# Output projection in three fp32r products at each weight chunk, with the routing of both token tiles in one piece behind it

## The chip, the cores and the metric

The kernel runs on one core of a Trainium2 chip, in one launch. The metric is device time in microseconds. A core has TensorE (PE; its weight loads are listed as PEld), VectorE (DVE), ScalarE (ACT), GpSimd (POOL) and SyncE (SP), which here only issues transfers. Each runs its own instructions in order, and they meet at semaphores. TensorE writes PSUM, eight banks of 512 fp32 columns, named `ps`.

## The reference, cut to what matters

256 tokens of width 1024 go through two layers. Layer 0 mixes tokens with a sparse attention of three branches, layer 1 with a block-sparse one; both end in a product with a 1024 x 1024 matrix, the output projection. After it come a layer norm, a router and a mixture of 16 experts, each token going to two of them.

```python
for layer in range(DEPTH):
    mix = mixer(x, w_in[layer], ...)            # ends in: o @ w_out
    x = layer_norm(DN_ALPHA * x + mix, ln_g[layer, 0], ln_b[layer, 0])
    ffn = grouped_moe(x, router_w, router_bias, w_gate[layer], w_up[layer], w_down[layer])
    x = layer_norm(DN_ALPHA * x + ffn, ln_g[layer, 1], ln_b[layer, 1])
```

`grouped_moe` takes the sigmoid of 16 router scores, picks the best of four groups by the sum of its two best biased scores, and in it the two best experts.

## The kernel before

Tokens lie in two tiles of 128 (index `a` or `t`, `T = 2`). A weight matrix is cut into units of 512 output columns (`UNIT`); a unit has eight chunks of 128 input rows (`KJ = 8`, index `j`). Weights pass through `ring`, eight slots of 2 MB, in the order of `STREAM`: the units of layer 0 (the output projection is units 5 and 6), 48 expert tiles, the units of layer 1 (output projection 13 and 14), 48 expert tiles. SyncE issues the load of an entry when the entry eight places earlier is used up (`wait_consumed`). For the first expert pairs this means: tiles 0 to 5 take slots of input units, tiles 6 and 7 those of the output projection, and tile 8 waits for `main.gate_done`, the end of the first pair's gate product.

**Input projection** (`project`). Operands are split in a high and a low fp32r part. For each chunk, ScalarE copies the weights to `wh` (`split_hi`), VectorE subtracts to get `wl` (`split_lo`), and TensorE makes three products for each token tile: high x high, high x low, low x high. `wh` and `wl` have three buffers (`WBUF`). `xh` and `xl` hold the split input.

**Attention** runs over items `m` (16 in layer 0, two to a pair of heads; 8 in layer 1, one to a pair). On TensorE, iteration `m` has `scores(m)`, `transpose_probs(m-2)` and `times_v(m-3)`. VectorE does the row maximum (`attention_max`, line 1128), `coefficients(m-1)`, one copy of the transposed probabilities (line 1344), and, when a pair of heads is finished, the copy of its output to `OT` (line 1352). ScalarE does four exponentials with sums (line 943) and the other copy of the transposed probabilities (line 952). GpSimd scales the probabilities (lines 1021 and 1022).

**Output projection** (`mix_out`, line 562) multiplies `OT` and the ring's weights as fp32, each matmul being two instructions of 512 columns, on top of a `seed` with the residual (line 569). Six chunks of the first unit come before the last head's `times_v`; then the rest of tile 0, then tile 1. Between the products of tile 1, TensorE transposes tile 0's normed rows (`transpose_tile`) and makes its router scores (`logits`, line 575):

```python
mix_out(l, 1, 0, range(KJ))
transpose_tile(0, R.xt, 4, lambda w: pe.wait_ge(N.x_ready, ready(2 * l, 0, w)))
mix_out(l, 1, 1, range(0, 4))
logits(l, 0)
mix_out(l, 1, 1, range(4, KJ))
```

**Routing** of a tile: VectorE takes statistics of each half row (`half_stats`, line 1173) and norms (`layer_norm`, lines 1177 to 1192, with a power on GpSimd, line 1026); ScalarE rounds the rows to `Xp[0]` (line 956) and GpSimd makes the low part `Xp[1]` (line 1031); both copy transposed rows; ScalarE makes the sigmoid (line 963); VectorE picks groups and experts (`choose`, lines 1204 to 1212), makes gate values (`gate_values`), turns counts of TensorE (`count_before`) into places (`places`) and writes a one-hot matrix `Pm`, a view of `wh[:, 0]` (`one_hot_tile`, line 1227). TensorE then gathers the rows (`gather_tile`, line 593), tile 0 first, tile 1 later, into the same banks, and the first expert pair's gate product follows (`to_hidden`, line 612).

Of the kernel before, what the change touches and what calls it, by code (L numbers as in the profile page):

```python
# [90 lines left out]
def build(nc, x, consts, w_in0, w_out0, cmp_kw1, cmp_kw2, cmp_vw1, cmp_vw2, cmp_kpos, cmp_vpos,  # L91
          w_in1, w_out1, router_w, router_b, w_gate, w_up, w_down, ln_g, ln_b, out):
    ctx = ExitStack()
    with ctx:
# [34 lines left out]
        def tiny(n):  # L129
# [5 lines left out]
        OT = [R6[:, 1536 + j * S:1536 + (j + 1) * S] for j in range(6)] + [R5[:, 2304 + j * S:2304 + (j + 1) * S] for j in range(2)]  # L135
# [68 lines left out]
                              "pt pt_sb pv ot_sb mix ln_in")  # L204
# [3 lines left out]
                   coef=16, scaled=16, pt=16, pt_sb=32, pv=16, ot_sb=8, mix=4, ln_in=32)]  # L208
# [9 lines left out]
        RT = namedtuple("RT", "xt xt_sb logits score sel pos hot table over xp xl ln_in")  # L218
        R = RT(*(sem(f"route_{n}") for n in RT._fields))
        rbase = [RT(*[0] * len(RT._fields)), RT(xt=4, xt_sb=4, logits=T, score=T, sel=T, pos=T, hot=1, table=1, over=1,  # L220
# [27 lines left out]
        def wait_consumed(eng, what):  # L248
# [13 lines left out]
        GATES = 5 * KJ  # L262
        chunk = lambda u, j: u * KJ + j if u < 5 else GATES + 1 + (u - 7) * KJ + j

        def wait_buffer(eng, c):
# [3 lines left out]
            if c == GATES:  # L269
                eng.wait_ge(L.proj, 11)  # L270
                return
            l, v, j = (0, c // KJ, c % KJ) if c < GATES else (1, (c - GATES - 1) // KJ, (c - GATES - 1) % KJ)
            if j == KJ - 1:
                eng.wait_ge(L.proj, base[l].proj + 2 * (v + 1))
            else:
                eng.wait_ge(w_used, (5 * l + v) * (KJ - 1) + j + 1)
# [132 lines left out]
        def _(pe):  # L409
# [125 lines left out]
            def attention(l):  # L535
                n = len(ITEMS[l])
                for m in range(n + 3):
# [6 lines left out]
                    else:  # L544
                        mix_out(l, 0, 0, range(0, 6))
# [9 lines left out]
            def mix_out(l, a, w, js):  # L555
                B, u = base[l], OUT[2 * l + w]
                for j in js:
                    if a == 0 and w == 0:
                        pe.wait_ge(L.ot_sb, B.ot_sb + j + 1)
                    if a == 0 and j % 4 == 0:  # L560
                        pe.wait_ge(*landing(("unit", u), j // 4))
                    last = mm(ps[:, 2 * a + w, :], OT[j][:, a * P:(a + 1) * P],  # L562
                              in_slot(("unit", u))[:, j * UNIT:(j + 1) * UNIT],
                              start=False, stop=(j == KJ - 1), skip_group_check=True)
                if j == KJ - 1:
# [853 lines left out]
```

## Time and profile before

| what | value |
|---|---|
| time, median of 3 runs | 820.42 us (819.17 to 820.86) |
| the profiled execution | 817.06 us, span 815.3 us |
| mean granted TensorE clock | 0.965 |
| TensorE, VectorE, ScalarE, GpSimd busy | 93%, 35%, 23%, 11% |
| HBM read | 243.35 MB |

The trace is one execution. In a row of a window the engines stand in the order PE, PEld, DVE, ACT, POOL. All times of events are microseconds from the start of its span. A matmul's listed duration overlaps that of its neighbours, so a rate is read from start to start. The granted clock is a share of 2.4 GHz and takes two levels, 1.00 and 0.50.

### The profile page before, as it was taken

Reading aid. Unit: us, or ns where it says so; the run is one execution under the profiler, and the core shown is the slowest. Engines: PE = TensorE matmul, PEld = TensorE weight load, DVE = VectorE, ACT = ScalarE, POOL = GpSimd, SP = SyncE. Lnnn points to the kernel's source line nnn. Section 1 sums busy time; section 2 is a strip of 40 time slices with the busy share of each in tenths; the row PEclk is TensorE's granted clock in tenths of the full one; section 3 lists DMA queues with packets and bytes.
Section 4 is the critical chain, followed back from the end, with each engine's and each line's share of the span. In section 5 each row is a group of like instructions: output and inputs, shape, how many; then the busy total and the mean of one; then the engine's idle time right before and its main releaser. Section 6 shows DMA issues by size and latency. Waiting matters only on the chain.

```text
span 815.3 us, 9027 instructions
## 1 busy us (share of the span) xinstructions
PE 754.2 (93%) x3713; PEld 402.3 (49%) x3713; DVE 282.5 (35%) x564; ACT 187.8 (23%) x435; POOL 88.0 (11%) x96
## 2 busy tenths in 40 slices
PE   5999999998999999998878999899899999998884
PEld 4877855545434444343236887555634344443331
DVE  3594365326212211111146874523521122111114
ACT  3443456312111001100004445612200110011000
POOL 0011234312000000000000320411200000000000
PEclk9999789999999999999997999999899999999997
DMA  9999400106599999999999854013489999999981
GB/s 297 366 391 411 188 1 2 52 15 243 201 430 427 428 429 426 428 427 427 429 388 386 328 207 174 34 52 110 148 353 427 428 428 425 430 427 428 428 347 53
DMA packets 38924, 245.03 MB, mean 301 GB/s; under 512 B 5344, under 2 KB 9568, under 8 KB 26592
## 3 DMA queue, kind: packets, MB, share of 16 engines
q1 hardware_dynamic: 38880, 244.41, 74.2%
q8 instruction: 32, 0.52, 0.3%
q14 instruction: 12, 0.10, 0.0%
HBM read 243.35 MB, written 1.05 MB: 300 GB/s over the span
## 4 chain that ended last, share of the span: by engine, by line
PE 79%; DMA 8%; DVE 7%; ACT 3%; issue 2%; POOL 0%; DVEq 0%; SPq 0%
PE ps L612 24%; PE ps L630 12%; DMA ring<-in_w_up 8%; PE ps L562 7%; PE ps L435 5%; PE ps L436 4%; PE ps L437 4%; PE ps L602 3%; PE ps L640 3%; PE ps L484 2%; ACT R L943 2%; PE ps L472 2%; PE ps L593 1%; PE ps L569 1%; PE ps L418 1%
## 5 line engine op out<-in xcount | busy, mean ns | idle before, releaser
L612 PE MATMUL ps<-ring,R 128*64 128x512 f32 x1024 | 229.9, 602 | 17.4 <-DMA ring<-in_w_up 7.9
L612 PEld LDWEIGHTS ps<-ring,R 128*64 128x64 f32 x1024 | 75.4, 138 | 150.6 <-issue 149.0
L630 PE MATMUL ps<-ring,R 128*64 128x512 f32 x512 | 113.4, 595 | 3.1 <-DVE R L1241 3.1
L841 ACT ACTIVATE wh<-ps,small 128x512 fp32r<-128x512 f32 x32 | 22.0, 687 | 276.1 <-PE ps L630 274.5
L1078 DVE TENSOR_TENSOR wl<-ring,wh 128x512 fp32r<-128x512 f32 x88 | 66.5, 770 | 48.3 <-ACT wh L819 48.1
L435 PE MATMUL ps<-wh,xh 128*128 128x512 f32 x176 | 71.9, 409 | 5.0 <-DVE wl L1078 4.9
L436 PE MATMUL ps<-wl,xh 128*128 128x512 f32 x176 | 70.4, 400 | 0.0
L437 PE MATMUL ps<-wh,xl 128*128 128x512 f32 x176 | 70.4, 400 | 0.0
L630 PEld LDWEIGHTS ps<-ring,R 128*64 128x64 f32 x512 | 35.3, 137 | 69.6 <-issue 64.0
L819 ACT CAST wh<-ring 128x512 fp32r<-128x512 f32 x88 | 54.3, 621 | 58.3 <-PE ps L437 58.3
L1249 DVE SCALAR_TENSOR_TENSOR wl<-ps,small,wh 128x512 fp32r<-128x512 f32 x32 | 24.0, 751 | 104.3 <-ACT wh L841 103.6
L562 PE MATMUL ps<-ring,R 128*128 128x512 f32 x128 | 56.8, 597 | 0.0
L1238 DVE TENSOR_TENSOR R<-R,ps 128x512 f32<-128x512 f32 x16 | 17.2, 1075 | 114.3 <-PE ps L612 114.3
L1245 DVE TENSOR_SCALAR wl<-ps 128x256 fp32r<-128x256 f32 x16 | 6.8, 424 | 115.4 <-PE ps L618 115.4
L943 ACT ACTIVATE R<-ps,small 128x128 f32<-128x128 f32 (+1 forms) x96 | 39.0, 419 | 29.7 <-DVE small L1128 29.7
L435 PEld LDWEIGHTS ps<-wh,xh 128*128 128x128 f32 x176 | 33.8, 192 | 15.0 <-DVE xl L1073 4.9
L986 POOL TENSOR_TENSOR R<-wh,small 128x512 f32<-128x512 f32 x8 | 8.3, 1043 | 284.6 <-PE ps L618 272.0
L437 PEld LDWEIGHTS ps<-wh,xl 128*128 128x128 f32 x176 | 33.6, 191 | 8.2
L436 PEld LDWEIGHTS ps<-wl,xh 128*128 128x128 f32 x176 | 33.8, 192 | 7.7
L562 PEld LDWEIGHTS ps<-ring,R 128*128 128x128 f32 x128 | 23.7, 190 | 27.6 <-issue 26.8
L1128 DVE TENSOR_REDUCE small<-ps 128x2 f32<-128x256 f32 (+1 forms) x48 | 24.5, 553 | 35.7 <-PE ps L472 35.7
L1011 POOL TENSOR_TENSOR R<-R 128x512 f32<-128x512 f32 (+1 forms) x16 | 23.3, 1459 | 123.9 <-DVE R L1121 123.9
(152 smaller groups left out, 812.9 us busy)
## 6 DMA issues: line engine op xcount, KB each, us to landing
ring<-in_w_gate SPq DMA_DIRECT2D x32, 2048.0 KB, 18.7
ring<-in_w_up SPq DMA_DIRECT2D x32, 2048.0 KB, 20.1
ring<-in_w_down SPq DMA_DIRECT2D x32, 2048.0 KB, 22.5
ring<-in_w_in SPq DMA_DIRECT2D x22, 1024.0 KB, 14.0
ring<-in_w_out SPq DMA_DIRECT2D x8, 1024.0 KB, 14.9
ring<-in_cmp_kw SPq DMA_DIRECT2D x2, 1024.0 KB, 16.3
ring<-in_cmp_vw SPq DMA_DIRECT2D x2, 1024.0 KB, 13.3
R<-in_ln_g SPq DMA_DIRECT2D x4, 512.0 KB, 5.1
```

Source lines behind the costliest of these rows:

```text
L435: mm(to, xh[:, j, tok], wh[:, c % WBUF], start=(j == 0), stop=False)
L436: mm(to, xh[:, j, tok], wl[:, c % WBUF], start=False, stop=False)
L437: last = mm(to, xl[:, j, tok], wh[:, c % WBUF], start=False, stop=(j == KJ - 1))
L562: last = mm(ps[:, 2 * a + w, :], OT[j][:, a * P:(a + 1) * P], in_slot(("unit", u))[:, j * UNIT:(j + 1) * UNIT], start=False, stop=(j == KJ ...
L602: last = mm(ps[:, bank, at * n:(at + 1) * n], Xp[k][:, a, j, :], Pm[:, a].rearrange("p e c -> p (e c)")[:, 0:n], start=(a == 0 and k == 0) ...
L612: last = mm(ps[64 * e:64 * e + 64, to, :], xe[:, j, at + 64 * e:at + 64 * e + 64], slots[e][:, j * UNIT:(j + 1) * UNIT], start=(j == 0), s ...
L630: last = mm(ps[64 * e:64 * e + 64, 2 + w, :], hT[:, k, 64 * e:64 * e + 64], slots[e][:, at:at + UNIT], start=(k == 0), stop=(k == FJ - 1))
L640: last = mm(ps[:, 4 + 2 * a + w, :], PmT[:, b, a, :], Yp[k][w], start=False, stop=(k == 1), skip_group_check=True)
L819: copy(wh[:, c % WBUF], in_slot(("unit", u))[:, j * UNIT:(j + 1) * UNIT]).then_inc(w_hi, 1)
L943: last = nc.scalar.activation(to, ps[:, 2 * (m % 2) + a, c:c + w], ACT.Exp, bias=nmax[:, m % 2, t, a:a + 1], accum_out=sums[:, m % 3, t, a ...
L1078: tt(wl[:, c % WBUF], in_slot(("unit", u))[:, j * UNIT:(j + 1) * UNIT], wh[:, c % WBUF], ALU.subtract).then_inc(w_lo, 1)
L1128: last = nc.vector.tensor_reduce(nmax[:, m % 2, t, :], ps[:, b:b + 2, t * P:t * P + (t + 1) * P], AX.X, ALU.max, negate=True)
```

## The change

The output projection is made like the input projection: weights split chunk by chunk in `wh` and `wl`, attention outputs split in two, three fp32r products for both token tiles at each chunk. `OT` is no longer fp32 space of its own but `xh` and `xl`. ScalarE writes the high part of a pair of heads (`out_hi`), VectorE the low part. The first three weight chunks are split during the last attention items. Three chunks (in place of six) come before the last `times_v`. A ring slot of an output unit is free when its last chunk is split. Tile 0 is transposed and routed behind all products; `choose`, `gate_values` and `places` work on both tiles at once, and the gathers of both tiles are in one piece (`gather`, which existed). `gather_tile`, `one_hot_tile` and the semaphore `hot` are gone.

```diff
-        OT = [R6[:, 1536 + j * S:1536 + (j + 1) * S] for j in range(6)] + [R5[:, 2304 + j * S:2304 + (j + 1) * S] for j in range(2)]
+        OT = [xh, xl]
...
-            elif n in OUT:
-                l, w = divmod(OUT.index(n), 2)
-                eng.wait_ge(L.mix, base[l].mix + T + w + 1)
             else:
                 eng.wait_ge(w_lo, chunk(n, KJ - 1) + 1)
...
-                        mix_out(l, 0, 0, range(0, 6))
+                        mix_out(l, 0, range(0, 3))
...
-            def mix_out(l, a, w, js):
+            def mix_out(l, w, js):
                 B, u = base[l], OUT[2 * l + w]
                 for j in js:
-                    if a == 0 and w == 0:
+                    c = chunk(u, j)
+                    if w == 0:
                         pe.wait_ge(L.ot_sb, B.ot_sb + j + 1)
-                    if a == 0 and j % 4 == 0:
-                        pe.wait_ge(*landing(("unit", u), j // 4))
-                    last = mm(ps[:, 2 * a + w, :], OT[j][:, a * P:(a + 1) * P],
-                              in_slot(("unit", u))[:, j * UNIT:(j + 1) * UNIT],
-                              start=False, stop=(j == KJ - 1), skip_group_check=True)
-                if j == KJ - 1:
-                    last.then_inc(L.mix, 1)
+                    pe.wait_ge(w_lo, c + 1)
+                    for a in range(T):
+                        to, tok = ps[:, 2 * a + w, :], slice(a * P, (a + 1) * P)
+                        mm(to, OT[0][:, j, tok], wh[:, c % WBUF], start=False, stop=False, skip_group_check=True)
+                        mm(to, OT[0][:, j, tok], wl[:, c % WBUF], start=False, stop=False, skip_group_check=True)
+                        last = mm(to, OT[1][:, j, tok], wh[:, c % WBUF], start=False, stop=(j == KJ - 1), skip_group_check=True)
+                        if j == KJ - 1:
+                            last.then_inc(L.mix, 1)
+                    if j < KJ - 1:
+                        last.then_inc(w_used, 1)
...
                 attention(l)
-                mix_out(l, 0, 0, range(6, KJ))
-                mix_out(l, 0, 1, range(KJ))
-                mix_out(l, 1, 0, range(KJ))
+                mix_out(l, 0, range(3, KJ))
+                mix_out(l, 1, range(KJ))
                 transpose_tile(0, R.xt, 4, lambda w: pe.wait_ge(N.x_ready, ready(2 * l, 0, w)))
-                mix_out(l, 1, 1, range(0, 4))
                 logits(l, 0)
-                mix_out(l, 1, 1, range(4, KJ))
-                pe.wait_ge(R.sel, C.sel + 1)
-                count_before(0)
                 for w in range(2):
                     seed(4 + w, 0, w, True)
                 transpose_tile(1, R.xt, 6, lambda w: pe.wait_ge(N.x_ready, ready(2 * l, 1, w)))
-                logits(l, 1)
-                pe.wait_ge(R.hot, C.hot + 1)
-                pe.wait_ge(R.xl, C.xl + 2)
-                for bank in range(4):
-                    gather_tile(bank, (2 * bank, 2 * bank + 1), 4 * SLOTS, 0)
+                logits(l, 1).then_inc(R.logits, 1)
                 seed(6, 1, 0, True)
-                pe.wait_ge(R.sel, C.sel + 2)
-                count_before(1)
+                pe.wait_ge(R.sel, C.sel + 1)
+                count_before()
                 pe.wait_ge(R.xl, C.xl + 2 * T)
...
+            def out_hi(l, m):
+                B, nb = base[l], BRANCHES[l]
+                if m >= 4 and (m - 4) % nb == nb - 1:
+                    act.wait_ge(L.pv, B.pv + m - 3)
+                    jq = (m - 4) // nb
+                    copy(OT[0][:, jq], ps[:, 6 + jq % 2, 0:S]).then_inc(L.ot_hi, 1)
...
                         copy(PTb[m % 2][:, 1, :], ps[:, 5, 0:3 * P]).then_inc(L.pt_sb, 1)
+                    out_hi(l, m)
+                    if n - 4 <= m < n - 1:
+                        split_hi(OUT[2 * l], m - n + 4)
+                for m in (n + 2, n + 3):
+                    out_hi(l, m)
+                for w in range(2):
+                    for j in range(3 - 3 * w, KJ):
+                        split_hi(OUT[2 * l + w], j)
...
                     if m >= 4 and (m - 4) % nb == nb - 1:
-                        dve.wait_ge(L.pv, B.pv + m - 3)
                         jq = (m - 4) // nb
-                        copy(OT[jq], ps[:, 6 + jq % 2, 0:S]).then_inc(L.ot_sb, 1)
-                half_stats(0, 0, 0, L.mix, B.mix + 1)
-                step(half_stats(0, 1, 0, L.mix, B.mix + 2))
+                        dve.wait_ge(L.ot_hi, B.ot_hi + jq + 1)
+                        tt(OT[1][:, jq], ps[:, 6 + jq % 2, 0:S], OT[0][:, jq], ALU.subtract).then_inc(L.ot_sb, 1)
+                    if n - 3 <= m < n:
+                        split_lo(OUT[2 * l], m - n + 3)
+                for w in range(2):
+                    for j in range(3 - 3 * w, KJ):
+                        split_lo(OUT[2 * l + w], j)
+                        if w and j == 3:
+                            half_stats(0, 0, 0, L.mix, B.mix + 1)
+                        if w and j == 5:
+                            half_stats(1, 0, 2, L.mix, B.mix + 2)
+                step(half_stats(0, 1, 0, L.mix, B.mix + 3))
                 layer_norm(2 * l, 0, 0, L.ln_in, B.ln_in + 32)
+                step(half_stats(1, 1, 2, L.mix, B.mix + 4))
                 transposed(xTr, 0, R.xt, C.xt, R.xt_sb)
-                half_stats(1, 0, 2, L.mix, B.mix + 3)
-                choose(C, 0)
-                step(half_stats(1, 1, 2, L.mix, B.mix + 4))
                 layer_norm(2 * l, 1, 2, L.ln_in, B.ln_in + 32)
-                places(C, 0)
-                one_hot_tile(0).then_inc(R.hot, 1)
                 transposed(xTr, 1, R.xt, C.xt, R.xt_sb)
-                step(gate_values(C, 0))
-                choose(C, 1)
-                gate_values(C, 1).then_inc(R.table, 1)
-                places(C, 1)
-                one_hot_tile(1).then_inc(main.onehot, 1)
+                choose(C)
+                gate_values(C)
+                places(C)
+                one_hot(main, slice(0, 4), 4)
```

`choose`, `gate_values` and `places` keep their instructions, each now over both tiles; `count_before` keeps its products and makes them together.

## Rows read from the trace of the kernel before

**Rows 1.** One window: length, five engines busy, PEclk, DMA share, GB/s.

```profile
213.00:413.00 200.00, 190.81 (x908) 78.51 (x906) 35.35 (x53) 17.91 (x28) 3.13 (x3) 0.99 1.00 423
```

**Rows 2.** SyncE in order of time; start us, us, line, what is transferred.

```profile
213.06 0.80 SPq L336 DMA_DIRECT2D ring<-in_w_up  x2
```

**Rows 3.** The chain that ended last, in order of time; start us, us, what.

```profile
158.87 5.35 PE ps L562 x12
165.64 15.65 PE ps L562 x36
...
182.16 3.44 PE ps L562 x8
...
187.28 3.54 PE ps L562 x8
190.85 0.71 DVE small L1173
...
196.12 1.96 PE ps L575 x16
...
200.80 1.71 PE ps L569 x2
203.88 2.12 PE ps L593 x16
206.00 7.02 PE ps L612 x32
...
483.11 0.87 PE ps L453 x8
495.18 0.88 PE ps L453 x8
...
569.57 0.71 DVE small L1173
...
574.83 3.60 PE ps L575 x16
...
586.08 7.02 PE ps L612 x32
```

**Rows 4.** Groups of the page: splits of weights, busy us and mean ns.

```profile
L1078 DVE TENSOR_TENSOR wl<-ring,wh 128x512 fp32r<-128x512 f32 x88 | 66.5, 770 | 48.3 <-ACT wh L819 48.1
...
L819 ACT CAST wh<-ring 128x512 fp32r<-128x512 f32 x88 | 54.3, 621 | 58.3 <-PE ps L437 58.3
```

**Rows 5.** ScalarE in layer 1's attention, in order of time.

```profile
524.61 0.37 ACT L943 ACTIVATE R<-ps,small 128x128 f32<-128x128 f32 x1 [1.20 <-DVE small L1128]
...
526.21 0.49 ACT L952 COPY R<-ps 128x384 f32<-128x384 f32 x1
527.59 0.37 ACT L943 ACTIVATE R<-ps,small 128x128 f32<-128x128 f32 x1 [0.89 <-DVE small L1128]
```

**Rows 6.** VectorE in the same stretch; in brackets idle time and releaser.

```profile
525.02 0.42 DVE L1352 COPY R<-ps 128x256 f32<-128x256 f32 x1
526.53 1.02 DVE L1128 TENSOR_REDUCE small<-ps 128x2 f32<-128x256 f32 x2 [1.10 <-PE ps L472]
```

**Rows 7.** VectorE in layer 0's tail, in order of time.

```profile
193.22 1.41 DVE L1192 SCALAR_TENSOR_TENSOR X<-X,small,R 128x512 f32<-128x512 f32 x2
...
200.50 0.18 DVE L1212 SCALAR_TENSOR_TENSOR small<-small 128x16 f32<-128x16 f32 x1
```

**Rows 8.** GpSimd in layer 0's tail.

```profile
192.06 0.56 POOL L1026 TENSOR_TENSOR small<-small 128x1 f32<-128x1 f32 x1 [7.11 <-DVE small L1178]
195.22 3.02 POOL L1031 TENSOR_TENSOR xl<-X,xh 128x512 fp32r<-128x512 f32 x2 [2.60 <-ACT xh L956]
```

**Rows 9.** Windows with TensorE's granted clock (the column PEclk).

```profile
199.00:202.00 3.00, 3.00 (x11) 2.27 (x11) 2.18 (x13) 0.00 (x0) 0.00 (x0) 0.50 0.63 240
424.00:427.00 3.00, 0.00 (x0) 0.00 (x0) 2.93 (x7) 0.00 (x0) 0.55 (x1) 1.00 1.05 386
428.00:437.00 9.00, 5.01 (x17) 3.85 (x18) 7.80 (x14) 3.89 (x7) 0.55 (x1) 0.50 1.05 386
```

More of the change, by code:

```diff
@@ L216, in ready @@
             return 2 * (k * T + t) + w + 1
-        RT = namedtuple("RT", "xt xt_sb logits score sel pos hot table over xp xl ln_in")
+        RT = namedtuple("RT", "xt xt_sb logits score sel pos table over xp xl ln_in")
         R = RT(*(sem(f"route_{n}") for n in RT._fields))
-        rbase = [RT(*[0] * len(RT._fields)), RT(xt=4, xt_sb=4, logits=T, score=T, sel=T, pos=T, hot=1, table=1, over=1,
+        rbase = [RT(*[0] * len(RT._fields)), RT(xt=4, xt_sb=4, logits=1, score=1, sel=1, pos=1, table=1, over=1,
                                                xp=2 * T, xl=2 * T, ln_in=32)]
@@ L268, in wait_buffer @@
                 return
-            if c == GATES:
+            u, j = CHUNKS[c]
+            if u == "gates":
                 eng.wait_ge(L.proj, 11)
-                return
-            l, v, j = (0, c // KJ, c % KJ) if c < GATES else (1, (c - GATES - 1) // KJ, (c - GATES - 1) % KJ)
-            if j == KJ - 1:
-                eng.wait_ge(L.proj, base[l].proj + 2 * (v + 1))
-            else:
-                eng.wait_ge(w_used, (5 * l + v) * (KJ - 1) + j + 1)
+            elif j < KJ - 1:
+                eng.wait_ge(w_used, sum(1 for v, i in CHUNKS[:c + 1] if v != "gates" and i < KJ - 1))
+            elif u in OUT:
+                l, w = divmod(OUT.index(u), 2)
+                eng.wait_ge(L.mix, base[l].mix + 2 * w + 2)
+            else:
+                l = int(u > 6)
+                eng.wait_ge(L.proj, base[l].proj + 2 * (u - U0[l] + 1))
         def ropes(l, n):
@@ L574, in logits, with count_before @@
                 for j in range(KJ):
-                    last = mm(ps[:, 7 * a, 0:E], xTr[:, j, a * P:(a + 1) * P], rw[:, j, :],
+                    last = mm(ps[:, 0, a * E:(a + 1) * E], xTr[:, j, a * P:(a + 1) * P], rw[:, j, :],
                               start=(j == 0), stop=(j == KJ - 1))
-                last.then_inc(R.logits, 1)
-            def count_before(a):
+                return last
+            def count_before():
                 before, ones = const("before"), const("ones")
-                if a == 0:
-                    mm(ps[:, 1, 0:E], before, sel[:, 0], start=True, stop=True).then_inc(R.pos, 1)
-                    return
+                mm(ps[:, 7, 0:E], before, sel[:, 0], start=True, stop=True)
                 mm(ps[:, 7, E:2 * E], before, sel[:, 1], start=True, stop=False)
@@ L588, in count_before @@
                 last.then_inc(R.pos, 1)
-            def gather_tile(bank, js, n, a):
-                for at, j in enumerate(js):
-                    for k in range(2):
-                        last = mm(ps[:, bank, at * n:(at + 1) * n], Xp[k][:, a, j, :],
-                                  Pm[:, a].rearrange("p e c -> p (e c)")[:, 0:n],
-                                  start=(at == 0 and a == 0 and k == 0), stop=(a == T - 1 and k == 1), skip_group_check=True)
-                return last
             def gather(rd, bank, js, n):
@@ new lines, in gate_values, with places @@
+            def gate_values(C):
+                dve.wait_ge(R.sel, C.sel + 1)
+                w = ch[:, 0:T * E].rearrange("p (a e) -> p a e", a=T)
+                step(tt(w, sc, sel, ALU.mult))
+                step(nc.vector.tensor_reduce(wsum, w, AX.X, ALU.add))
+                step(nc.vector.reciprocal(wsum, wsum))
+                tt(gate, w, bc(wsum, 2, E), ALU.mult).then_inc(R.table, 1)
+            def places(C):
+                dve.wait_ge(R.pos, C.pos + 1)
+                step(stt(pos, ps[:, 7, 0:T * E].rearrange("p (a e) -> p a e", a=T), 1.0, sel, ALU.add, ALU.mult))
```

47 lines of the change are left out of this document (19 added, 28 removed).

## The prediction

> **What bounds the kernel now.** I read the page first, then the chain of waits, then the stretches between its landmarks. The busy shares say TensorE (93%), but a share doesn't say what a microsecond is worth in each stage, so I asked for the windows. From 213 to 413 us, the expert stage of layer 0, the DMA share is 1.00 at 423 GB/s [rows 1]: forty expert weight tiles of 2 MB pass in 200 us, 5.0 us each, while TensorE has gaps. The ring holds eight tiles, and tile 8 may only be fetched when the first pair's gate product has freed two slots. SyncE issues it at 213.06 us [rows 2], the instant that product ends (206.00 + 7.02 [rows 3]). Layer 1 repeats the pattern from 586.08 [rows 3]. So each expert stage is a rigid block of transfers that begins with the end of the first gate product. The reader should see what follows: whatever moves the start of that product (206.00 and 586.08) moves the end of the kernel one for one, twice. Ahead of it runs one chain: attention, output projection, layer norm, routing, gathers. Earlier fetches of tiles 6 and 7, which the change allows, buy nothing: those two are loaded long before they are used, and tile 8 waits for the gate product all the same.
>
> The sum goes in four terms per layer, then the clock. "Tail" is the time from the last product of the output projection to the start of the gate product: 206.00 - 190.83 = 15.2 us in layer 0 and 586.08 - 569.55 = 16.5 us in layer 1 [rows 3].
>
> **Products.** Today a layer has 32 fp32 matmuls, two instructions each, in 5.35 + 15.65 + 3.44 + 3.54 = 28.0 us [rows 3]. The change has 96 fp32r matmuls of the form of the input projection. There, the time from one pair of head transposes to the next is 495.18 - 483.11 = 12.07 us, of which 0.87 is the transposes; (12.07 - 0.87)/48 = 0.233 us each. 96 x 0.233 = 22.4 us: **-5.6 us a layer**. The split of weights must keep up: 0.62 us on ScalarE and 0.77 on VectorE per chunk [rows 4] against 6 x 0.233 = 1.40 on TensorE, so it does, as in the input projection.
>
> **Work taken out of the projection.** Tile 0's transposes and logits ran between products: 187.28 - 181.29 - 3.44 = 2.55 us. They go behind the last product: **-2.55**.
>
> **A bubble before chunk 3.** ScalarE splits chunks 0 to 2 ahead of time, but then stands at the last head's `out_hi`, which waits for the last `times_v`. Chunk 3's split is queued behind it. TensorE idles through one output copy (about 0.4, an estimate below the 0.49 us copy of 384 columns [rows 5]), one weight copy (0.62) and one subtraction (0.77), a little overlapped and with hand-overs: **+1.9**. If the three chunks didn't exist it would be no shorter, so below zero is excluded; the upper end is 2.5.
>
> **Attention slips.** VectorE copied each head's output (0.41 us at 525.02) freely. Now it must wait until ScalarE has done the four exponentials and a copy, then `out_hi`. In layer 1: exponentials from 524.61, copy until 526.70, `out_hi` until 527.1, subtraction until 527.5. Behind the waiting subtraction stands the next item's maximum, which today starts at 526.53 and releases the next exponentials at 527.59 [rows 5, 6]. It starts 1.0 us late. This binds each of layer 1's last four items, and VectorE also puts three weight splits of 0.77 us in front of maxima and the last coefficients. In layer 0 an output ends only every second item, and TensorE's own chain of the following item absorbs the wait. Followed item by item the slip is up to 1.4 us in layer 0 and 3.9 in layer 1; the lower end, if TensorE's queue covers everything, is 0. I take **+1.0 and +3.2**, nearer to what the schedule shows.
>
> The last product therefore ends 5.25 us earlier in layer 0 and 3.05 in layer 1.
>
> **The tail at full clock.** Today layer norm, transposes, choice and gather of tile 0 lie under tile 1's products. Now both tiles finish 0.7 us apart and everything is behind them. With t as the last product of tile 1: tile 0's statistics start at t - 0.7 and its rows are ready 3.7 us later (190.85 [rows 3] to the end of the pair from 193.22 [rows 7], today). Then VectorE has a statistic (0.7) and a transposed copy (0.7). GpSimd is the next queue: it takes 3.02 us for the low parts of tile 0's rows, which ScalarE's copies release, and only then computes the 0.56 us root for tile 1 [rows 8]. So tile 1's first half is ready near t + 8.05; TensorE, which has tile 0's logits (1.96) and two seeds (2 x 28.0/32 = 1.75) queued ahead, gets to its transposes at t + 8.2. Today they come at t + 3.2: +5.0. On the other side TensorE had a tile gather and a seed between logits and counts: the choice was made at 200.68 but the seed ended at 200.80 + 1.71 = 202.51 [rows 3, 7]. That cover goes: -1.8. Then the choice on doubled widths +0.25 (estimate from its eleven instructions, most bound by their fixed time), one more count +0.15, a one-hot of 512 instead of 256 columns +0.25 (both estimates), and 16 more gather matmuls, at most 2.12 us as those from 203.88 [rows 3], of which I take 1.75 for the overlap at the end. Net +5.6 against layer 0's tail: **20.8 us**, that is +5.6 and +4.3. The SyncE queue adds no wait here: its layer norm loads were issued earlier than they are needed. ScalarE's table load for the sigmoid ends before the logits.
>
> So far: layer 0 -5.25 + 5.6 = +0.35, layer 1 -3.05 + 4.3 = +1.25. Together +1.6.
>
> **The clock.** This decides the case. In layer 0 the granted clock is 0.50, its 1.2 GHz level, from 199 us, after TensorE had only transposes, the 16-column logits and short gaps, the last until 196.12; between the layers it is idle from 424 to 427 at full clock, and then at 0.50 from 428 to 437, although it had work in more than half of that time [rows 9]. Work at that level costs what rows show: logits 3.60 us instead of 1.96, a seed 1.71 [rows 3] instead of 28.0/32 = 0.87. The new tail has an idle 2.5 us right after the products and then only transposes, logits, seeds and counts with gaps. So I expect 0.50 from about 3 to 4 us into the tail. Tile 0's logits (+1.6) and seeds (+1.7) then push tile 1's transposes later, by 2.9 of these 3.3; tile 1's logits half the time (+0.8); count and transposes +0.4; the gathers, at up to twice 0.13 us each until the clock is back, +1.8. **+5.9 a layer**. The lower end is 0 (clock holds), the upper one 9.7 (all at half: 3.3 + 1.6 + 1.0 + 3.8).
>
> The Trainium skill ("TensorE: Matmul & The Clock Gate", section on HAM oscillation) names gaps in which the engine is idle as what throttles it. Read so, short gaps with work between them do nothing; the trace shows otherwise, 0.50 at 199 us with TensorE at work since 196.12. By that reading the sum would stay without this term, the first rival below.
>
> **Sum.** Layer 0: +0.35 + 5.9 = +6.25; layer 1: +1.25 + 5.9 = +7.15; together +13.4. The profiled execution took 817.06 us (span 815.3 and 1.8 around it), 3.4 below the median of the timed runs. The difference carries over: 820.42 + 13.4 = **833.8 us**.
>
> **Rivals.**
> The clock holds through the tail. For it: in layer 0 it came back soon, sixteen gathers in 2.12 us from 203.88, and the new tail has two dense seeds in its middle. Against: [rows 9]. Then the sum is +1.6: 822.0 us, not slower by measurement. It decides up to a tail of 20.8 us; each microsecond more, in both layers, is two in the end. Chance 0.15, of which 0.04 on the faster side and 0.08 within the measurement.
> The slip in attention is absorbed (TensorE's queue covers VectorE's wait), the clock falls. For: VectorE is idle 1.1 us before a maximum [rows 6]. Against: layer 1, where each late item has the wait. 13.4 - 4.2 = +9.2: 829.6 us. Chance 0.17.
> The clock stays low through all gathers and into the gate product: 3 us more per layer. For: the 9 us of low clock between the layers [rows 9]. Against: the gathers are dense work. 839.8 us. Chance 0.12.
> The change does not lengthen the tail as told, because GpSimd and TensorE's queue do not hold tile 1 back: -2 per layer, 829.8. Chance 0.06. The forecast itself has 0.50, with a range of its own of 829 to 838.
>
> What can be told from no change is about 0.2%, 1.6 us: faster below 818.8, slower above 822.1. From the cases (the first rival's share, and 0.02 and 0.03 for sizes that I have wrong in the others): faster 0.06, same 0.11, slower 0.83. The range takes in the forecast, the last three rivals and the upper part of the first: 821 to 841 us; what it leaves out is some 0.1 below and 0.05 above.
>
> **What the changed profile would show.** Product groups at the new line with 0.23 us from start to start. VectorE's maxima of late items released by the subtraction, and layer 1's items 4 us apart instead of 3.1. An idle stretch of about 2 us before chunk 3. A tail of 26 to 28 us to the first gate product. Granted clock 0.50 in the middle of it. GpSimd's root for tile 1 behind the low parts of tile 0. The transfers of tile 8 later by 6 and 13 us. The prediction is wrong if the clock stays at 1.00 in the tail, if the last product ends much more than 5 us earlier, or if expert transfers no longer run at a share of 1.00.

## The result, and the profile after

| | before | after |
|---|---|---|
| time, median of 4 runs | 820.64 us (819.17 to 820.92) | 833.64 us (832.12 to 834.56) |
| the profiled execution, its span | 817.06, 815.3 us | 832.12, 830.3 us |
| mean granted TensorE clock | 0.965 | 0.950 |

The ratio is 1.0168, with a 95% interval from 1.0148 to 1.0188: the change makes the kernel slower, where 833.8 us were forecast. In the profile after, the output projection stands at lines 567 to 569, statistics at 1176, the norm's two steps at 1185 and 1195, logits at 582, a seed at 576, counts at 588 to 592, gathers at 599, the gate product at 609.

The chain that ended last, after, in order of time (start us, us, what). It answers to [rows 3].

```profile
184.88 0.24 PE ps L567
185.12 0.23 PE ps L568
...
185.62 0.71 DVE small L1176
...
190.94 3.40 PE ps L582 x16
194.34 3.60 PE ps L576 x4
...
199.70 2.06 PE ps L582 x16
...
207.43 5.91 PE ps L599 x32
213.33 7.02 PE ps L609 x32
...
583.27 3.60 PE ps L576 x4
...
596.36 6.00 PE ps L599 x32
602.36 7.02 PE ps L609 x32
```

The first gate product starts at 213.33 in place of 206.00 and at 602.36 in place of 586.08. Tile 0's logits (3.40 us, 1.96 at full clock), the seeds (3.60 and 1.81) and the gathers (5.91 and 3.97) are stretched; tile 1's logits, at 2.06, are not. The times at full clock are those of the kernel with fill products below. SyncE's queue says the same of the transfers: tile 8, at 213.06 before [rows 2], is issued behind that gate product.

```profile
220.39 0.80 SPq L339 DMA_DIRECT2D ring<-in_w_up  x2
```

Windows after, with the granted clock in the third column from the end; they answer to [rows 1, 9].

```profile
164.00:167.00 3.00, 1.21 (x5) 0.74 (x5) 1.96 (x4) 1.93 (x4) 0.00 (x0) 1.00 0.00 0
167.00:171.00 4.00, 4.00 (x12) 3.09 (x12) 1.05 (x2) 0.70 (x2) 0.00 (x0) 0.57 0.00 0
...
191.00:199.00 8.00, 7.92 (x28) 5.51 (x28) 2.94 (x7) 2.03 (x3) 4.04 (x4) 0.57 0.35 120
199.00:201.00 2.00, 1.30 (x12) 1.30 (x12) 0.65 (x1) 1.98 (x3) 0.81 (x1) 1.00 0.11 45
201.00:211.00 10.00, 7.87 (x35) 6.16 (x36) 4.68 (x19) 0.61 (x2) 1.74 (x2) 0.52 0.00 0
222.00:422.00 200.00, 189.54 (x902) 78.44 (x900) 35.25 (x52) 17.31 (x27) 3.13 (x3) 0.99 1.00 425
```

The reader should see three things. The expert stage still runs at a DMA share of 1.00, so it is the same rigid block, only later. The clock is low in most of the tail, with TensorE listed busy 7.92 of 8 us. And it is low once more where the prediction had nothing: at 167 to 171 us, in the middle of dense products, behind the idle stretch before chunk 3.

ScalarE and then VectorE in layer 1's attention; they answer to [rows 5, 6].

```profile
533.87 0.37 ACT L938 ACTIVATE R<-ps,small 128x128 f32<-128x128 f32 x1 [0.90 <-DVE small L1131]
...
535.83 0.40 ACT L814 CAST xh<-ps 128x256 fp32r<-128x256 f32 x1
536.09 0.66 ACT L807 CAST wh<-ring 128x512 fp32r<-128x512 f32 x1
538.25 0.37 ACT L938 ACTIVATE R<-ps,small 128x128 f32<-128x128 f32 x1 [1.50 <-DVE small L1131]
```

```profile
536.26 0.42 DVE L1353 TENSOR_TENSOR xl<-ps,xh 128x256 fp32r<-128x256 f32 x1 [1.90 <-ACT xh L814]
536.60 0.68 DVE L1081 TENSOR_TENSOR wl<-ring,wh 128x512 fp32r<-128x512 f32 x1
537.20 1.02 DVE L1131 TENSOR_REDUCE small<-ps 128x2 f32<-128x256 f32 x2
```

The wait goes round: the subtraction waits 1.90 us for ScalarE's `out_hi`, the maximum stands behind it and a weight split, and ScalarE's next exponential waits for the maximum. The items are 4.38 us apart, and 3.0 to 3.3 before.

Layer 0's tail on GpSimd, and VectorE's norm of tile 1 that waits for it; they answer to [rows 7, 8].

```profile
189.98 3.03 POOL L1034 TENSOR_TENSOR xl<-X,xh 128x512 fp32r<-128x512 f32 x2 [2.59 <-ACT xh L959]
192.97 0.56 POOL L1029 TENSOR_TENSOR small<-small 128x1 f32<-128x1 f32 x1
```

```profile
193.56 1.41 DVE L1195 SCALAR_TENSOR_TENSOR X<-X,small,R 128x512 f32<-128x512 f32 x2 [1.05 <-POOL small L1029]
```

**Where the time went.** I follow the start of the gate product. Layer 0: 213.33 - 206.00 = +7.33. Part of that difference has nothing to do with the change. Attention of layer 0 begins 1.3 us earlier in the profiled execution after; the two executions are 1.2 us apart already at 25 us, inside the input projection, which both kernels share. There the clock stays at 0.50 until 14.7 us in the execution before, and is 1.00 from 10.3 us in the one after. TensorE's first instruction of attention, before and then after:

```profile
93.00 0.82 PE L468 MATMUL ps<-causalb,identb 128*128 128x384 bf16 x2 [0.38 <-ACT R L832]
```

```profile
91.71 0.82 PE L471 MATMUL ps<-causalb,identb 128*128 128x384 bf16 x2 [0.38 <-ACT R L827]
```

From there to the projection it is 66.9 us in place of 65.8, so attention slips by 1.1. The projection, to the end of its last product (186.29 in place of 190.82), is 27.7 us in place of 32.0, -4.3, and the tail is 27.0 us in place of 15.2, +11.9. Together -1.3 + 1.1 - 4.3 + 11.9, which is the +7.33 within rounding. Layer 1: attention begins 8.50 later (the 7.33 and 1.17 from the stages between); then attention +3.2, projection 25.4 us in place of 31.35, -5.9, and tail 27.05 in place of 16.5, +10.5: together +7.78 of its own. Layer 1's expert stage gives back 1.2. 7.33 + 1.17 + 7.78 - 1.2 = +15.1, the difference of the profiled executions.

### The profile page after: what moved, and what is told of

Same layout as the page of the kernel before. It is cut to its first block, busy times and chain, and to the rows that moved or that the text cites. A ratio compares the mean times of both kernels' runs of the same rounds, so it can differ in the third digit from the quotient of the medians.

```text
span 830.3 us, 9217 instructions
## 1 busy us (share of the span) xinstructions
PE 754.5 (91%) x3777; PEld 422.0 (51%) x3777; DVE 295.3 (36%) x562; ACT 210.6 (25%) x481; POOL 88.4 (11%) x96
## 4 chain that ended last, share of the span: by engine, by line
PE 73%; DMA 12%; DVE 8%; ACT 3%; issue 2%; POOL 0%; SPq 0%; DVEq 0%
PE ps L609 22%; PE ps L627 11%; DMA ring<-in_w_up 8%; PE ps L438 4%; PE ps L439 4%; PE ps L440 4%; PE ps L599 4%; DMA ring<-in_w_down 4%; PE ps L637 2%; ACT R L938 2%; PE ps L567 2%; PE ps L568 2%; PE ps L569 2%; PE ps L576 2%; PE ps L475 1%
## 5 line engine op out<-in xcount | busy, mean ns | idle before, releaser
L609 PE MATMUL ps<-ring,R 128*64 128x512 f32 x1024 | 228.5, 599 | 17.9 <-DMA ring<-in_w_up 10.5
L1081 DVE TENSOR_TENSOR wl<-ring,wh 128x512 fp32r<-128x512 f32 x120 | 88.4, 750 | 62.3 <-ACT wh L807 61.6
L807 ACT CAST wh<-ring 128x512 fp32r<-128x512 f32 x120 | 73.9, 623 | 76.2 <-PE ps L440 57.6
L599 PE MATMUL ps<-wh,xh 128*128 128x256 f32 x128 | 37.4, 321 | 2.2 <-DVE wh L1231 2.2
L440 PEld LDWEIGHTS ps<-wh,xl 128*128 128x128 f32 x176 | 33.5, 190 | 8.2
L833 ACT ACTIVATE R<-ps 128x512 f32<-128x512 f32 x16 | 9.6, 597 | 104.9 <-PE ps L609 104.9
L599 PE MATMUL ps<-wh,xl 128*128 128x256 f32 x128 | 34.5, 300 | 0.0
```

The lines of the kernel that those rows point to most:

```text
L440: last = mm(to, xl[:, j, tok], wh[:, c % WBUF], start=False, stop=(j == KJ - 1))
L599: last = mm(ps[:, bank, at * n:(at + 1) * n], Xp[k][:, a, j, :], Pm[:, a].rearrange("p e c -> p (e c)")[:, 0:n], start=(a == 0 and k == 0) ...
L609: last = mm(ps[64 * e:64 * e + 64, to, :], xe[:, j, at + 64 * e:at + 64 * e + 64], slots[e][:, j * UNIT:(j + 1) * UNIT], start=(j == 0), s ...
L807: copy(wh[:, c % WBUF], in_slot(("unit", u))[:, j * UNIT:(j + 1) * UNIT]).then_inc(w_hi, 1)
L1081: tt(wl[:, c % WBUF], in_slot(("unit", u))[:, j * UNIT:(j + 1) * UNIT], wh[:, c % WBUF], ALU.subtract).then_inc(w_lo, 1)
```

## Experiments

Ratios are against runs of the kernel before on the same chip (its median 820.4 to 821.1 us there).

| kernel | median us | ratio (95%) |
|---|---|---|
| before's products, routing behind | 839.47 | 1.0205 (1.0172 to 1.0238) |
| the same with fill products | 826.42 | 1.0069 (1.0039 to 1.0099) |
| after with fill products | 824.36 | 1.0042 (1.0013 to 1.0072) |
| after, seeds late | 833.58 | 1.0152 (1.0108 to 1.0196) |
| after, chunk 3 split early | 830.09 | 1.0106 (1.0076 to 1.0137) |
| after, maxima first | 830.31 | 1.0125 (1.0086 to 1.0165) |
| after, fill, early, first | 817.39 | 0.9968 (0.9946 to 0.9990) |
| the same, seeds late, root first | 826.01 | 1.0080 (1.0053 to 1.0108) |
| the same, root first only | 820.42 | 0.9995 (0.9962 to 1.0027) |
| the same, seeds late only | 821.95 | 1.0017 (0.9988 to 1.0046) |
| before with fill products | 813.30 | 0.9923 (0.9899 to 0.9946) |

A fill product is 128 x 384 in bf16, from two constants into a PSUM bank that nobody reads: it adds computation, and no kernel leaves any out.

**Routing behind, products as before.** The change cut in two: `mix_out` stays fp32, the routing part of the diff is made.

```diff
                 mix_out(l, 1, 0, range(KJ))
+                mix_out(l, 1, 1, range(KJ))
                 transpose_tile(0, ...)
-                mix_out(l, 1, 1, range(0, 4))
                 logits(l, 0)
-                mix_out(l, 1, 1, range(4, KJ))
```

> The second half of the change alone: the fp32 output projection of the kernel before (its own order, no split weights, no waits in attention), but both tiles normed after the last product and routed in one piece. My theory (the tail behind the products, lengthened by half clock, is the loss, and the fp32r products are a gain that is smaller): the last product ends 2.55 us earlier in each layer, the tail grows from 15.2 and 16.5 to about 28 us, together +19: 839 us, 835 to 843, slower than the changed kernel. Rival (the loss lies in the products' part: VectorE's wait in attention, the bubble before chunk 3, and the routing in one piece costs nothing since TensorE idles anyway): about the time of the kernel before, 819 to 823 us.

It took 839.47 us (836.11 to 840.62). The rival falls. The order of the work alone costs 19 us by the medians, and 14 to 19.5 by the interval of the ratio. What the fp32r products give back is smaller and not well measured: 5.8 us by the medians, but the intervals of the two ratios overlap. The terms of the prediction without tail and clock, 2 x (5.6 - 1.9) - 1.0 - 3.2, give 3.2. The chain in layer 0:

```profile
196.65 3.59 PE ps L575 x16
206.33 1.97 PE ps L575 x16
213.98 6.29 PE ps L592 x32
220.27 7.02 PE ps L602 x32
```

**Fill products in the changed kernel.** This takes the clock away and leaves the rest.

```diff
                 mix_out(l, 1, range(KJ))
+                fill(6, 12)
                 transpose_tile(0, ...)
+                fill(6, 4)
                 logits(l, 0)
...
+                fill(1, 4)
                 logits(l, 1).then_inc(R.logits, 1)
                 seed(6, 1, 0, True)
+                fill(1, 12)
...
                 count_before()
+                fill(1, 6)
```

> The changed kernel with products of no use (identity by mask, bf16, 384 columns, 12 + 4 + 4 + 12 + 6 of them a layer) put where TensorE idles in the tail; they write banks that nobody reads. My theory (half clock costs some 6 us of each tail): the granted clock holds near 1.00 for most of the tail, tails shrink from 27.2 to 21 to 23 us, 10 us less: 823.5 us, 821 to 827. Rival (the tail is as long as its serial chain of norm, transposes, logits and choice, and the clock is incidental): unchanged or 1 to 2 us slower by the extra products, 833 to 836 us.

824.36 us (818.35 to 827.94). The chain in layer 0's tail, whose clock is 1.00 throughout:

```profile
195.30 1.96 PE ps L586 x16
197.26 1.81 PE ps L576 x4
199.07 1.00 PE ps L421 x8
200.83 1.96 PE ps L586 x16
...
207.84 3.97 PE ps L603 x32
```

Logits 1.96 for 3.40, seeds 1.81 for 3.60, gathers 3.97 for 5.91. From the end of the last product (190.63 and 572.34) to the gate product (211.75 and 593.48) it is 21.1 us in both layers, where 27.0 were without them: the clock is worth 5.9 us a layer in the tail. The low clock behind the idle stretch before chunk 3 lies ahead of the fill products and is still there (from 171.2 us).

**The same fill products with the fp32 products**, the last corner of the square.

> The kernel before with its fp32 products and the routing of both tiles in one piece behind them (839.47 alone), and the same fill products in the gaps that brought the changed kernel from 833.64 to 824.36. It fills the last corner of a square: routing beside or behind the products, with the clock held in both. Theory: moving the routing costs the price of the order itself, whatever the clock does. Held clock took 9.3 us from the changed kernel, so it takes as much here: 839.5 - 9.3 = 830.2 us (828 to 833), and against the kernel before with its own fill products (813.3) the order alone costs some 17 us, 8.4 a layer. The predicted terms read for held clocks give less: 813.3 + 2 x (5.6 + 3.5 - 2.55) = 826.4. Rival: the products as fp32 leave the clock high by themselves, the loss behind them is smaller and so is the gain of the fill: 835 us or more.

826.42 us (821.73 to 833.21). I had put 830.2 first and 826.4, from the predicted terms read for held clocks, second: the second came out. The clock is 1.00 in both tails. The fill products took 13.0 us away here by the medians, more than the 9.3 in the changed kernel. With held clocks the order costs 826.4 - 813.3 = 13.1 us by the medians (813.3 is the kernel before with fill products, below); the kernels ran on different chips, and the ratios to before give 12.

**Seeds late.** The prediction had tile 1 wait behind the seeds, so I took these away from there.

```diff
-                for w in range(2):
-                    seed(4 + w, 0, w, True)
...
-                seed(6, 1, 0, True)
...
-                        seed(7, 1, 1, True)
+                        for w in range(2):
+                            seed(4 + w, 0, w, True)
+                            seed(6 + w, 1, w, True)
```

> The changed kernel with the three seeds of the expert sum (tile 0's two and tile 1's first) moved behind the first pair's up product, where the transfers and not TensorE set the pace. My theory (tile 0's seeds at half clock keep tile 1's transposes waiting): transposes of tile 1 follow its rows, 2.9 us earlier in each layer, 828 us, 826 to 830; a part may be lost again, since less dense work leaves the clock low longer. Rival (GpSimd's root or ScalarE's copies bound tile 1 anyway, TensorE's queue is no bound): within 1 us of 833.6.

833.58 us (832.19 to 838.45). No gain, but not for the rival's reason. TensorE in layer 0's tail; in brackets its idle time and what ended it:

```profile
195.71 1.97 PE L421 MATMUL ps<-cst,X 128*128 128x128 f32 x8 [0.22 <-DVE X L1194]
198.47 3.60 PE L582 MATMUL ps<-rw,R 128*128 128x16 f32 x16 [0.78 <-DVE R L1061]
204.99 0.61 PE L588 MATMUL ps<-small,cst 128*128 128x16 f32 x2 [2.92 <-DVE small L1215]
```

Tile 1's transposes do come right behind its rows, 5.6 us after the start of tile 0's where they came 8.95 us after. But the clock stayed at its half level, from 192.7 to 213.2 us: tile 1's logits take 3.60 us and not 2.06. In the changed kernel it came back at 198.0, at the end of the seeds, for one stretch. So the seeds cost 3.6 us there, and they are also the dense work that brings the clock back.

**Chunk 3 split early.** Chunks 3 to 5 are split ahead of the last head's output copy, on both engines.

```diff
-                for m in (n + 2, n + 3):
-                    out_hi(l, m)
+                out_hi(l, n + 2)
+                for j in range(3, 6):
+                    split_hi(OUT[2 * l], j)
+                out_hi(l, n + 3)
```

> The changed kernel with chunks 3 to 5 of the first output unit split before the last head's output is copied, on ScalarE and VectorE. My theory: the bubble of 1.9 us before chunk 3 goes in both layers, and with it the stretch of half clock that follows it in layer 0 (1.7 us): 5 us less, 828.5 us, 827 to 830.5. Rival (the same subtraction is then late for the last chunk, or the bubble is covered because transfers are what ends last): within 1 us of 833.6.

830.09 us (828.71 to 832.69): the gain is there, 3.5 of the 5 expected. No idle stretch, and no low clock behind it. In layer 0 the projection is 3.4 us shorter and in layer 1 1.8, but the low clock of the tail begins earlier, and the tails are 0.7 and 1.4 us longer:

```profile
166.00:171.00 5.00, 5.00 (x23) 4.00 (x22) 2.46 (x4) 2.25 (x4) 0.00 (x0) 1.00 0.36 79
185.00:191.00 6.00, 5.12 (x23) 4.73 (x24) 4.59 (x9) 3.04 (x4) 3.54 (x3) 0.50 0.25 107
```

**Maxima first.** VectorE's low part and weight splits go behind the next item's maximum and coefficients.

```diff
                     if 1 <= m <= n:
                         coefficients(l, m - 1)
+                    out_lo(m - 1)
```

(`out_lo` holds the subtraction for the output and the weight split. It is called one iteration late.)

> The changed kernel with VectorE's low part of a finished head pair, and the weight splits of the last attention items, put behind the next item's maximum and coefficients. My theory (in layer 1 the maximum stands behind a subtraction that waits for ScalarE, 3.2 us of slip): layer 1's items are 3.1 to 3.3 us apart again, 3.2 us less: 830.4 us, 829 to 832; in layer 0 nothing. Rival (the slip comes from ScalarE's own extra work or from the three weight splits on VectorE wherever they stand): within 1 us of 833.6.

830.31 us (828.25 to 831.60), the number that was expected, but the trace doesn't bear out the reason. ScalarE and TensorE in layer 1's attention:

```profile
535.28 0.37 ACT L938 ACTIVATE R<-ps,small 128x128 f32<-128x128 f32 x1 [0.89 <-DVE small L1131]
...
539.05 0.37 ACT L938 ACTIVATE R<-ps,small 128x128 f32<-128x128 f32 x1 [0.89 <-DVE small L1131]
```

```profile
539.55 0.65 PE L504 MATMUL ps<-R 128*64 128x256 f32 x4 [0.81 <-DVE xl L1341]
```

The late items are 3.77 us apart, not 3.1 to 3.3: now TensorE's `times_v` waits for the low part, which comes later. From the start of layer 1's attention to the projection it is 32.7 us, for 33.3 in the changed kernel and 30.15 before, so VectorE's order is 0.7 of the 3.2 us; the rest stays in either order. In layer 0, where nothing was expected, 0.9 of the 1.1 us came back (66.0 for 66.9). Both readings repeat in the other profiles: in layer 1 30.1 to 30.6 us in the four kernels without the split, 33.3 to 33.5 in three with VectorE's first order, 32.5 to 32.7 in four with the maxima first (all of them with 3.4 us of low clock in it; the two profiles without have 32.7 with the first order and 31.4 with the maxima first). The low clock behind the idle stretch moved from layer 0 to layer 1 and cancels. The remaining 1.7 of the 3.3 us are in part the tails, 0.4 us shorter each; why isn't settled.

**All three together.**

> The changed kernel with the products of no use that hold the clock (as in the kernel with the dense fill), chunks 3 to 5 split early and the maximum first. If the terms add up (fill 824.4, chunk 3 early -3.5, maximum first -3.2): 817.7 us, 816 to 820, a little faster than before. Rival (they overlap: part of what chunk 3 early gives is clock, which the fill holds already): 819 to 821.

817.39 us (814.10 to 821.05), and faster than before, by 0.1 to 0.5%. The window from 166 to 222 us, the clock at 1.00:

```profile
166.00:222.00 56.00, 54.89 (x292) 34.44 (x292) 25.85 (x54) 16.08 (x22) 8.19 (x7) 1.00 0.43 163
```

**With seeds late and GpSimd's root first as well.** The root for tile 1 goes ahead of the low parts of tile 0. Two more fill products stand where tile 0's seeds stood, and three where tile 1's first stood.

```diff
                         tt(rstd[:, t:t + 1], ve[:, t:t + 1], half[:, t:t + 1], ALU.pow).then_inc(N.rstd, 1)
+                    for t in range(T):
                         if k == 2 * l:
```

> As the kernel with fill and orders, and also the seeds behind the first up product and GpSimd's root for tile 1 ahead of the low parts of tile 0. At full clock the seeds no longer bring the clock back, the fill does it, and tile 1's transposes can follow its rows: 1.3 us less in each layer than with fill and orders, 815 us, 813.5 to 818. Rival (the chain of norm and copies bounds tile 1 just the same): equal to it.

826.01 us (822.36 to 829.20): 8.6 more than without the two edits, where 1.3 less a layer was expected. The theory fell. From the first fill product to the gate product it is 25.7 and 25.3 us, for 21.3 without the edits: 8.4 us. There were two suspects, so each edit was made alone.

Root first alone:

> The kernel with fill products and both changed orders (817.39), and one order more: GpSimd's root for tile 1 ahead of the low parts of tile 0. It differs from the kernel that lost 8.6 us by the seeds alone, which stand here where they stood. Theory: the seeds, that is dense work between the two tiles, carried the loss there, because without them the granted clock fell. Here the clock holds. VectorE's two norm instructions for tile 1 take some 3.4 us in place of 1.41, since GpSimd now works beside them, but start 1.1 us earlier, so tile 1's rows come about 0.8 us later: 817.4 + 2 x 0.8 = 819.0 us (817.4 to 820.5), granted clock 1.00 through the tail. Rival: VectorE slowed beside GpSimd is what cost the time, through the gap that it leaves on TensorE ahead of the transposes of tile 1, and the clock falls here too: 823 to 826 us.

Seeds late alone:

> The kernel with fill products and both changed orders (817.39), with the seeds of the expert banks moved behind the first pair's up product and three more fill products where the last seed stood; GpSimd's order is left alone. Theory (the seeds are what kept the clock, the place of GpSimd's root matters little): TensorE stands about 1 us idle ahead of tile 1's transposes, the granted clock falls to 0.50 in tile 1's part, tile 1's logits take 3.5 us in place of 1.96 and the fill products behind them end after the choice: 3 to 4 us a layer, 824.5 us (822.5 to 826.5). Rival (the slowed VectorE was the cause): the clock holds, tile 1's rows are ready as before, and the time is that of the kernel with the seeds in place within 1.5: 816 to 819 us.

They took 820.42 us (814.65 to 825.82) and 821.95 (815.99 to 826.60, a little below the expected range). Their intervals overlap with each other's, and the profiled executions are 2 us behind the one with neither edit before the first tail begins, so the verdict rests on the tails in the traces, from one execution each. VectorE and GpSimd with the root first:

```profile
190.21 1.40 DVE L1197 SCALAR_TENSOR_TENSOR X<-ps,small,R 128x512 f32<-128x512 f32 x2
191.53 3.36 DVE L1207 SCALAR_TENSOR_TENSOR X<-X,small,R 128x512 f32<-128x512 f32 x2
```

```profile
190.90 6.86 POOL L1046 TENSOR_TENSOR xl<-X,xh 128x512 fp32r<-128x512 f32 x4
```

VectorE's second step has 3.36 us beside GpSimd's low parts, for 1.41 us without them. From the first fill product to the gate product it is 22.1 us, and 21.3 with the old order: 0.8 a layer, the theory's figure, and the clock is 1.00 through both tails. (The medians differ by 3.0 us, more than these 1.7.) The Trainium skill ("GPSIMD Engine Reference", section "Specifications") says that the two engines share their SBUF interfaces, which collide when VectorE has two SBUF inputs. The trace agrees: the step with both inputs in SBUF is the slow one.

The window from 193 to 205 us, first with the root first, then with the seeds late:

```profile
193.00:205.00 12.00, 11.13 (x73) 7.56 (x72) 6.95 (x21) 4.36 (x5) 5.80 (x4) 1.00 0.29 89
```

```profile
193.00:205.00 12.00, 11.75 (x54) 8.48 (x55) 4.57 (x18) 4.15 (x5) 3.03 (x2) 0.57 0.29 87
```

TensorE in the latter, just ahead of that window and into it:

```profile
191.63 0.48 PE L581 MATMUL ps<-causalb,identb 128*128 128x384 bf16 x2
193.24 1.78 PE L421 MATMUL ps<-cst,X 128*128 128x128 f32 x8 [1.13 <-DVE X L1206]
194.81 1.49 PE L581 MATMUL ps<-causalb,identb 128*128 128x384 bf16 x4
```

Two short fill products and 1.13 us idle stand in the place of four seed instructions (1.96 us), and the clock falls at 193.8 us, in spite of the fills around; in layer 1 it falls too, for 3.4 us. From fill to gate product it is 25.0 us in layer 0 and 22.3 in layer 1, for 21.3: 4.7 us in all. The medians differ by 4.6, the ratios by 4.0. The listed busy share doesn't warn: it is higher in the window of low clock. With both edits the clock falls in both layers for 10 us, and the loss, 8.4 us, is more than the 1.7 and 4.7 of the single ones.

**Fill products in the kernel before.** Six ahead of tile 1's transposes, four ahead of its logits.

```diff
+                fill(6, 6)
                 transpose_tile(1, R.xt, 6, ...)
+                fill(2, 4)
                 logits(l, 1)
```

> The kernel before with ten products of no use a layer (six ahead of tile 1's transposes, four ahead of its logits). My theory (in the tail of the kernel before too the clock falls, for 3.4 us in layer 0 and 6.4 in layer 1): with the clock held, 1.4 and 2.7 us less, 816.6 us, 815 to 819. Rival (the fall there is off the path or not prevented): 820.6 within 1 us.

813.30 us (811.99 to 818.58), the best of all, and 3.3 less than the 816.6 expected. TensorE in layer 0's tail:

```profile
196.91 1.32 PE L418 MATMUL ps<-cst,X 128*128 128x128 f32 x8 [0.28 <-DVE X L1198]
198.07 0.81 PE L574 MATMUL ps<-causalb,identb 128*128 128x384 bf16 x4
199.01 1.96 PE L579 MATMUL ps<-rw,R 128*128 128x16 f32 x16
```

From the last half's statistics to the gate product it is 13.6 us in both layers (193.75 to 207.35, 572.13 to 585.74), for 15.2 and 16.5 before. These 4.5 us are what the traces show of the 7.1, and close to the 1.4 and 2.7 expected. The profiled execution, at 816.8, is 3.5 above its median; it enters layer 0's attention at 95.89 us in place of 93.00, with a longer stretch of low clock ahead of it, where the kernels are the same. Where the other 2.6 us lie isn't settled.

## Why the prediction was right, and where it was not

**The bound.** Right. The gate product's start carries to the end one for one: +7.33 and +7.78 of its own give 15.1, with 1.2 lost and 1.2 given back between. The transfers of tile 8 are 7.3 and 16.3 us later, where 6 and 13 were forecast.

**Products.** Right: 0.23 us from start to start. Layer 1's projection is 5.9 us shorter, for 5.6 + 2.55 - 1.9 = 6.25.

**The bubble.** The idle stretch was predicted at 1.9 and is 1.79 (layer 0) and 1.80 us (layer 1). What it does to the clock was not foreseen: in layer 0 the products from 167.3 to 170.7 us are 0.43 us apart in place of 0.23, about 1.5 us in all. Splitting chunk 3 early took away both. In layer 1 an idle stretch of the same length left the clock at 1.00.

**Attention slips.** Right in both layers: +1.1 in layer 0, where 1.0 was taken, and +3.2 in layer 1, as predicted. The ends alone hide it in layer 0: the projection starts at 158.61 and at 158.79 before, because the execution after entered attention 1.3 us earlier. The same lengths come back in the other profiles (those whose first item takes 9.2 us): 65.8 without the split, 66.9 with it. The cause named is right for layer 0, where the other order of VectorE gave back 0.9, and only in part for layer 1, where it gave back 0.7. The rival in which the slip is absorbed falls.

**The other rivals.** The clock stays low through most of the gathers (to 211.7 us in layer 0), but not in the gate product, which takes its 7.02 us: the rival with 3 us more a layer falls. So does the one in which tile 1 isn't held back.

**The tail at full clock.** Predicted 20.8 us, measured 21.1 with fill products. The queueing was as told: transposes of tile 1 8.4 us behind the last product (predicted 8.2). That also bears out the first rival's sum of 822.0 us: with the clock held in the tail it was 824.4, and 833.6 less twice 5.9 would be 821.9.

**The clock.** Predicted +5.9 a layer, measured 5.9. Logits and seeds of tile 0 carry 1.44 and 1.8, the gathers 1.9. Tile 1's logits, at +0.8 in the sum, cost 0.1: the clock had come back with the seeds. The prediction weighed a rule of the Trainium skill ("TensorE: Matmul & The Clock Gate", HAM oscillation), by which gaps throttle the engine. The trace agrees that a gap can do it, and shows that its length alone doesn't decide: an idle stretch of 1.8 us between dense products was followed by the low clock in layer 0 and not in layer 1, and with the maxima first in layer 1 and not in layer 0.

**The sum, and what was luck.** The sum was +13.4. The medians give +13.0, and the interval of the ratio 12.1 to 15.4. In the traces the parts that the change moved give +8.6 in layer 0 (forecast +6.25) and +7.8 in layer 1 (forecast +7.15), 3.0 more than forecast. The term that was too small is the projection of layer 0: -4.3 in place of -5.6 - 2.55 + 1.9 = -6.25, mostly because the prediction put the low clock behind the idle stretch at nothing, which costs 1.5 us. The tails were 0.3 to 0.4 too small, and layer 1's projection gave 5.9 of 6.25. That the profiled executions differ by 15.1 and not by more is the 1.3 us by which the one after was ahead at the start of attention. The medians differ by less still: the step "the difference carries over" was 2.1 too large, since before's profiled execution was 3.6 below its median, after's only 1.5. So the mechanism was right, and that the forecast is within 0.2 us is luck.

**What the square of four kernels shows.** Of the 18.9 us that the order costs with fp32 products, 13.1 stay where the clock is held in both orders. The other 5.8 are the clock: it costs the kernel with the routing behind 13.0 us, and the kernel before 7.1. With fp32r products and the routing behind it costs 9.3.

**Left open.** At full clock the fp32r kernel has 21.1 us of tail and before 13.6; with everything mended it is still 4 us behind before with fill products. A version with fp32r products and tile 0 routed between them wasn't made. Why the same bubble lowers the clock in one layer and not in the other isn't settled either, nor what holds the 2.5 us of slip that stay in layer 1's attention.

## What to carry to other kernels

Work that lies under another tile's products is free only there: count what comes out from under cover before the saving on the products. Price a tail of small dependent steps at half the clock, look for what dense work stands in it, and try a few products that nobody reads: ten a layer made the kernel before 0.8% faster. Where a copy is split over two engines, try the waiting half behind whatever the next item needs; here it gave back 1.6 of 4.3 us. Before two traces are compared by their times, look for a place ahead of the change: the executions here were 1.2 us apart in code that both kernels share.

## What the runs showed of the hardware that was not expected

- The clock fell with TensorE listed busy: 0.57 in a window with 11.75 of 12 us busy, 1.00 in one with 11.13.
- Behind 1.79 us idle between dense products the clock was down for 3.4 us in layer 0; behind 1.80 us in layer 1 it was not. With the maxima first it was the other way round.
- Two of VectorE's 128 x 512 steps with both inputs in SBUF: 1.41 us alone, 3.36 beside GpSimd. GpSimd's four took 6.86 us, where two pairs took 3.04 and 3.03.
- Executions of one kernel differ by several us: 9.6 between the fastest and the slowest of 10 of the changed kernel with fill products, and of the kernel before 4.4 among 19 on one chip, 9.2 among 24 on another. Whether fill products make the times less even isn't shown. The low clock between 80 and 110 us (0.72 before, 0.66 in the profile of before with fill products) is one place where executions differ: layer 0's first attention item takes 12.2 us in four of the profiles and 9.2 in the others.
